# Regrouping VectorE's attention steps, output projections in rounds, and paired norms of 256 columns, in a three-layer block on one core

## The reference

```python
# layers 0 and 1
u = rms_norm(x) @ w_in                     # 256 x 2560
# layer 0: retention, 6 heads;  layer 1: differential attention, 6 heads of 2 maps
p = softmax(q k^T * scale + bias);  a = p[0] - lam * p[1];  o = a @ v
o_mem = memory_attention(...)              # 4 heads of 64, keys from mem
x = x + concat([o_main, o_mem]) @ w_out    # 1024 x 1024
x = x + (silu(gate) * up) @ w_down         # 2816 wide
# layer 2 (the second block): an SSD mixer and a "fox" attention side by side
y_ssd = ssd_mixer(...)   # 16 heads of 64: scores = (C B^T) * decay, times x * dt
y_fox = fox_mixer(...)   # 16 heads of 64: q and k normed per head, causal softmax, @ v
x = x + concat([y_ssd, y_fox]) @ w_out     # 2048 x 1024, then a convolved gated MLP
```

## Time and profile before

| | before |
|---|---|
| median of 3 runs | 1086.97 us (1084.75 to 1086.97) |
| profiled execution, its own time | 1086.96 us |
| its span, first to last instruction | 1085.1 us |
| PE busy | 1049.3 us, 97% |
| DVE / ACT / POOL busy | 761.3 / 587.0 / 176.6 us |
| mean granted TensorE clock | 0.995 |
| chain that ended last | PE 81%, DVE 12%, ACT 3% |

### The profile page before, as it was taken

One profiled execution on the slowest core, in us unless ns is written; L12 is line 12 of the kernel. 1 busy time (PEld: TensorE's weight loads), 2 busy tenths in 40 slices (PEclk: granted clock), 3 DMA queues, 4 the chain that ended last, 5 costly groups with the idle time before them and its releaser, 6 DMA issues.

```text
span 1085.1 us, 23877 instructions
## 1 busy us (share of the span) xinstructions
PE 1049.3 (97%) x8638; PEld 1011.4 (93%) x8638; DVE 761.3 (70%) x1324; ACT 587.0 (54%) x1047; POOL 176.6 (16%) x184
## 2 busy tenths in 40 slices
PE   6999999999999997999999999999899999999998
PEld 6989899999999886899999998999788999999998
DVE  6876685666555887876666548868877679988843
ACT  7654564444545654654445446665555466666532
POOL 3100121111010000411111110000211033444300
PEclk9999999999999999999999999999999999999999
DMA  8533455555665421555555664544233355555563
GB/s 291 176 131 108 142 176 179 184 183 173 191 179 175 135 85 54 180 189 176 188 177 170 193 198 140 175 136 137 83 113 91 124 194 177 191 175 187 165 204 104
DMA packets 51479, 174.43 MB, mean 161 GB/s; under 512 B 5840, under 2 KB 7120, under 8 KB 51280
## 3 DMA queue, kind: packets, MB, share of 16 engines
q1 hardware_dynamic: 51408, 173.46, 49.4%
HBM read 172.39 MB, written 1.05 MB: 160 GB/s over the span
## 4 chain that ended last, share of the span: by engine, by line
PE 81%; DVE 12%; ACT 3%; issue 2%; POOL 1%; DMA 1%; SPq 0%; DVEq 0%; ACTq 0%; POOLq 0%
PE bank L685 24%; PE bank L686 23%; PE bank L687 23%; DVE ring_lo L1482 4%; DVE xw_lo L1488 1%; PE bank L668 1%; PE bank L670 1%; PE bank L669 1%; ACT tmp L1239 1%; ACT tmp L1298 1%; PE bank L802 1%; DMA ring_raw<-w_kv 1%; DVE x L1580 1%; PE bank L793 0%; DVE tmp L1855 0%
## 5 line engine op out<-in xcount | busy, mean ns | idle before, releaser
L685 PE MATMUL bank<-xw_hi,ring_hi 128*128 128x256 f32 x1576 | 453.3, 288 | 2.7 <-DVE ring_lo L1482 1.5
L686 PE MATMUL bank<-xw_lo,ring_hi 128*128 128x256 f32 x1576 | 446.4, 283 | 0.0
L687 PE MATMUL bank<-xw_hi,ring_lo 128*128 128x256 f32 x1576 | 446.3, 283 | 0.0
L1482 DVE TENSOR_TENSOR ring_lo<-ring_raw,ring_hi 128x1024 fp32r<-128x1024 f32 (+2 forms) x338 | 402.4, 1194 | 56.5 <-ACT ring_hi L1057 50.8
L1057 ACT ACTIVATE ring_hi<-ring_raw 128x1024 fp32r<-128x1024 f32 (+2 forms) x338 | 341.1, 1012 | 88.8 <-PE bank L687 84.7
L685 PEld LDWEIGHTS bank<-xw_hi,ring_hi 128*128 128x128 f32 x1576 | 302.6, 192 | 9.8 <-issue 5.1
L686 PEld LDWEIGHTS bank<-xw_lo,ring_hi 128*128 128x128 f32 x1576 | 302.7, 192 | 0.2
L687 PEld LDWEIGHTS bank<-xw_hi,ring_lo 128*128 128x128 f32 x1576 | 302.7, 192 | 0.0
L685 PE MATMUL bank<-act_hi,ring_hi 128*128 128x256 f32 x736 | 212.1, 288 | 12.2 <-DVE ring_lo L1898 7.8
L686 PE MATMUL bank<-act_lo,ring_hi 128*128 128x256 f32 x736 | 210.1, 285 | 0.0
L687 PE MATMUL bank<-act_hi,ring_lo 128*128 128x256 f32 x736 | 210.0, 285 | 0.0
(11 more groups left out here) (199 smaller groups left out, 1168.8 us busy)
## 6 DMA issues: line engine op xcount, KB each, us to landing
ring_raw<-w_up SPq DMA_DIRECT2D x132, 512.0 KB, 3.2
ring_raw<-w_in SPq DMA_DIRECT2D x85, 512.0 KB, 3.3
ring_raw<-w_down SPq DMA_DIRECT2D x48, 512.0 KB, 3.7
ring_raw<-w_down SPq DMA_DIRECT2D x24, 384.0 KB, 3.8
ring_raw<-w_ob SPq DMA_DIRECT2D x10, 512.0 KB, 3.5
ring_raw<-w_oa SPq DMA_DIRECT2D x16, 256.0 KB, 2.7
ring_raw<-w_oa SPq DMA_DIRECT2D x8, 512.0 KB, 3.6
ring_raw<-w_kv SPq DMA_DIRECT2D x7, 512.0 KB, 6.3
```

The lines of the kernel that those rows point to most:

```text
L685: mm(bank[b][:, 0:T], w_hi, tile(hi, t), start=kk == 0, stop=False)
L686: mm(bank[b][:, 0:T], w_hi, tile(lo, t), start=False, stop=False)
L687: last = mm(bank[b][:, 0:T], w_lo, tile(hi, t), start=False, stop=end)
L1482: V.tensor_tensor(ring_lo[:, a:b], ring_raw[:, a:b], ring_hi[:, a:b].bitcast(f32), SUB).then_inc(lo_done, 1)
```

## The change

- **Output projection in rounds (layers 0 and 1).** `oa` and `ob` become one stage `oc` of eight full slots. A slot is a pair of inputs and a half (four) of the output tiles, in the order of `ROUNDS`. All eight outputs accumulate in banks 0 to 3 (two to a bank) until the fourth pair; then `x` is added once, 512 columns at a time (`rounds_into_stream`). Half 1 uses banks 2 and 3, and waits for the last scores.
- **Differential softmax (layer 1).** VectorE no longer scales the second map: it folds the factors into one small operation and makes the difference in one pass; ScalarE applies the common factor.
- **Memory and fox outputs.** ScalarE copies them from PSUM straight to `act_hi` and VectorE writes `act_lo` from PSUM, in place of a VectorE copy, a ScalarE copy and a GpSimd subtraction. Their `mix` steps go.
- **Fox softmax (layer 2).** Two reductions over both heads in place of four (banks 2 and 3 become one tensor `scores2`); ScalarE normalises in place of VectorE.
- **SSD weights.** The time step is multiplied into `x_tok` in two operations (`ssd_steps`); then one product for a pair of heads replaces four smaller ones.
- **Query and key norms of layer 2.** A query pair and a key pair share one chain of 256 columns (`pair_squares`, `pair_norm`, `pair_spread`, `pair_out`); fox scores start one slot later.

The diff, cut to its core:

```diff
 PHASES = [("kv", 8, [8], 4),
-          ("in0", 20, [8], 20), ("oa0", 8, [6], 8), ("ob0", 2, [8], 2), ("up0", 44, [8], 4), ("down0", 24, [8, 8, 6], 12),
-          ("in1", 20, [8], 20), ("oa1", 8, [4], 8), ("ob1", 4, [8], 4), ("up1", 44, [8], 4), ("down1", 24, [8, 8, 6], 12),
+          ("in0", 20, [8], 20), ("oc0", 8, [8], 8), ("up0", 44, [8], 4), ("down0", 24, [8, 8, 6], 12),
+          ("in1", 20, [8], 20), ("oc1", 8, [8], 8), ("up1", 44, [8], 4), ("down1", 24, [8, 8, 6], 12),
           ("in2", 45, [8], 45), ("oa2", 16, [8, 4], 16), ("ob2", 4, [8], 4), ("up2", 44, [8], 4), ("down2", 24, [8, 8, 6], 12)]
...
+ROUNDS = {"oc0": [(0, 0), (1, 0), (0, 1), (1, 1), (2, 0), (3, 0), (2, 1), (3, 1)],
+          "oc1": [(0, 0), (1, 0), (0, 1), (1, 1), (2, 0), (2, 1), (3, 0), (3, 1)]}
...
-    norm(1, 23, 10 + 64, True)
+    norm(1, 22, 10 + 64, True)
...
-    for k, slot in ((6, 11), (7, 11), (0, 19), (1, 19), (2, 23), (3, 23), (4, 26), (5, 26)):
+    for k, slot in ((0, 19), (1, 19), (2, 23), (3, 23), (4, 25), (5, 25)):
...
+        at(2, a + 2, "ssd_weights", p)
         for n in range(2):
-            at(2, a + n + 1, "ssd_weights", 2 * p + n)
             at(2, a + n, "ssd_decay", 2 * p + n)
+    at(2, 16, "ssd_steps", 0)
+    at(2, 18, "ssd_steps", 1)
     for j in range(4):
         a = 21 + 6 * j
-        norm(2, a + 2, 20 + 2 * j)
-        norm(2, a + 4, 28 + 2 * j)
+        at(2, a + 2, "pair_squares", j, 0)
+        at(2, a + 4, "pair_squares", j, 1)
+        at(2, a + 5, "pair_norm", j)
+        for which in range(2):
+            plan[2][a + 6 + which].insert(0, ("pair_spread", j, which))
+            plan[2][a + 7 + which].insert(0, ("pair_out", j, which))
         for n in range(2):
-            p, slot = 2 * j + n, a + 7 + 3 * n
+            p, slot = 2 * j + n, a + 8 + 3 * n
             at(2, slot, "fox_scores", p)
             plan[2][slot + 1].insert(0, ("fox_probs", p))
             at(2, slot + 2, "fox_weights", p)
             at(2, slot + 3, "fox_values", p)
-            at(2, slot + 4, "mix", 8 + p)
...
+        def mixed(layer, k):
+            if layer < 2 and k >= 6:
+                return sm_out, number["fill", (layer, 12 + k)] + 1
+            if layer == 2 and k >= 8:
+                return fx_out, k - 7
+            return mix_lo, number["mix", (layer, k)] + 1
...
+            def project_rounds(layer, then, halfway):
+                ph = PH[f"oc{layer}"]
+                for c, (pair, half) in enumerate(ROUNDS[ph.name]):
+                    slot, g = ph.tile(0, c)
+                    pe.wait_ge(lo_done, g + 1)
+                    if pair == 0 and half == 1:
+                        if layer == 0:
+                            pe.wait_ge(sm_e, 4)
+                            pe.wait_ge(r_pt, RET_HEADS)
+                        else:
+                            pe.wait_ge(sm_m, so_far["scores"])
...
+                        if pair == 3 and j == 1:
+                            last.then_inc(ob_done, 1)
+                    last.then_inc(tile_done, 1)
+                    then(c)
...
+            def rounds_into_stream(layer, q, after):
+                ph = PH[f"oc{layer}"]
+                for c, (pair, half) in enumerate(ROUNDS[ph.name]):
+                    split_hi(ph, 0, c)
+                    after(ph, 0, c)
+                    if pair == 3:
+                        for p in (2 * half, 2 * half + 1):
+                            act.wait_ge(out_ready, ph.out0 + p + 1)
+                            stream_hi(q, 2 * p, x)
+                            stream_hi(q, 2 * p + 1, x)
+                            stream_square(q, 2 * p, x)
+                            stream_square(q, 2 * p + 1, x)
...
+            def softmax(layer, kind, h, m):
+                if kind != "diff" or m == 0:
+                    return
+                n = number["scores", (layer, kind, h, m)]
+                act.wait_ge(diffed, h + 1)
+                p, c0 = probs(n), 2 * ((n - 1) % 2)
+                for it, (a, width) in enumerate([(0, P), (P, T)]):
+                    last = A(p[:, a:a + width], p[:, a:a + width], ACT.Copy, scale=rrow[:, c0 + it:c0 + it + 1])
+                last.then_inc(sm_d, 1)
+            def values(layer, kind, h):
+                t, full = filled(layer, kind, h)
+                if kind != "mem" or not full:
+                    return
+                act.wait_ge(sm_o, number["weights", (layer, kind, h)] + 1)
+                A(tile(act_hi, t - 12), bank[6][:, 0:T], ACT.Copy).then_inc(vals_hi, 1)
...
+            def fox_probs(layer, p):
+                act.wait_ge(fx_r, p + 1)
+                for n in range(2):
+                    for it, (a, width) in enumerate([(0, P), (P, T)]):
+                        w_ = fox_p(n)[:, a:a + width]
+                        last = A(w_, w_, ACT.Copy, scale=rrow[:, 2 * n + it:2 * n + it + 1])
+                last.then_inc(fx_n, 1)
+            def fox_values(layer, p):
+                act.wait_ge(fx_o, p + 1)
+                A(tile(act_hi, 8 + p), bank[6][:, 0:T], ACT.Copy).then_inc(fx_hi, 1)
...
+            def rounds_into_stream(layer, q, early, middle, late):
+                ph = PH[f"oc{layer}"]
+                late_split = []
+                for c, (pair, half) in enumerate(ROUNDS[ph.name]):
+                    early(ph, 0, c)
+                    if pair == 3:
+                        for p in (2 * half, 2 * half + 1):
...
+                            two_out = x[:, 2 * p * T:(2 * p + 2) * T]
+                            V.tensor_tensor(two_out, two_out, bank[p][:, :], ADD).then_inc(out_ready, 1)
+                            stream_lo(q, 2 * p, x)
+                            stream_lo(q, 2 * p + 1, x)
+                    middle(ph, 0, c)
+                    late_split.append(c)
+                    if not (c == 6 and pair == 3):
+                        for d in late_split:
+                            split_lo(ph, 0, d)
+                        late_split = []
+                    late(ph, 0, c)
...
+            def pair_norm(layer, j):
+                n, y = pair_no(j), normed(0)[:, 0:T]
+                v = newton_step(n, y)
+                V.scalar_tensor_tensor(y, v, -3.0, y, ADD, MUL).then_inc(np_nt, 1)
+                dve.wait_ge(np_nt, 5 * n + 3)
+                dve.wait_ge(np_bc, PAIRS_FROM + 2 * j)
+                root_split(n, y, T)
+            def pair_out(layer, j, which):
+                dve.wait_ge(np_bc, PAIRS_FROM + 2 * j + which + 1)
+                t = 20 + 8 * which + 2 * j
+                V.scalar_tensor_tensor(u[:, t * T:(t + 2) * T], u[:, t * T:(t + 2) * T], pcol(("foxq", "foxk")[which]),
+                                       bank[4][:, :], MUL, MUL).then_inc(np_out, 1)
...
-                    small_op(V.tensor_scalar(rrow[:, c:c + 2], rrow[:, c:c + 2], lam[:, 4:5], None, MUL))
-                    small_op(*[V.tensor_scalar(p[:, a:a + width], p[:, a:a + width], rrow[:, c + it:c + it + 1], None, MUL)
-                               for it, (a, width) in enumerate([(0, P), (P, T)])])
                     first, c0 = probs(n - 1), 2 * ((n - 1) % 2)
+                    small_op(V.scalar_tensor_tensor(rrow[:, c:c + 2], rowsum[:, c0:c0 + 2], lam[:, 4:5], rrow[:, c:c + 2],
+                                                    MUL, MUL))
                     for it, (a, width) in enumerate([(0, P), (P, T)]):
-                        last = V.scalar_tensor_tensor(p[:, a:a + width], first[:, a:a + width],
-                                                      rrow[:, c0 + it:c0 + it + 1], p[:, a:a + width], MUL, ADD)
-                    last.then_inc(sm_n, 1)
+                        last = V.scalar_tensor_tensor(p[:, a:a + width], p[:, a:a + width],
+                                                      rrow[:, c + it:c + it + 1], first[:, a:a + width], MUL, ADD)
+                    last.then_inc(diffed, 1)
...
+            def ssd_weights(layer, p):
+                if p == 0:
                     dve.wait_ge(cb_done, 2)
-                dve.wait_ge(ss_e, h + 1)
-                g = h // 8
-                for tt, (a, width) in enumerate([(0, T), (T, P)]):
-                    k = 16 * tt + h
-                    last = V.scalar_tensor_tensor(s[:, a:a + width], s[:, a:a + width], tok_dt[:, k:k + 1],
-                                                  cb[:, g * 384 + a:g * 384 + a + width], MUL, MUL)
-                last.then_inc(ss_p, 1)
+                dve.wait_ge(ss_e, 2 * p + 2)
+                s = ssd_pair(p).rearrange("p (n c) -> p n c", n=2)
+                g = p // 4
+                V.tensor_tensor(s, s, cb[:, g * 384:(g + 1) * 384].unsqueeze(1).to_broadcast([P, 2, 384]), MUL).then_inc(ss_p, 1)
+            def ssd_steps(layer, g):
+                if g == 0:
+                    dve.wait_ge(act_small, 7)
+                    dve.wait_ge(tr_out, so_far["turn"])
+                xg = x_tok[:, :].rearrange("p (t h d) -> p t h d", t=2, h=16)[:, :, 8 * g:8 * g + 8, :]
```

(18 more changed lines are left out.)

210 lines of the change are left out of this document (148 added, 62 removed).

## The result

The changed kernel takes 1089.76 us (median of 7 runs, 1088.53 to 1090.69); the kernel before takes 1086.97 (median of 7, 1084.07 to 1087.40). The ratio over all these executions is 1.0034, with a 95% interval of 1.0022 to 1.0046 (the medians alone give 1.0026): 0.34% slower, where 1.0% faster was forecast. The profiled execution took 1090.28 us.

A forecast was written before the change was run, and what follows sets the result against it. TensorE's steady matmul stream was taken as the bound, leaving about 18 us of PE waits and 5 us of clock falls; gains less tail and other costs sum to -10.7 us from 1086.96, giving 1076.3 us, range 1072 to 1081.

The forecast's parts named there:

- Heads of the rounds (-1.1, -1.7): Layer 0's first round needs only inputs 6 and 7: `act_lo` wait gone, -1.1 us, and the clock's fall behind it, -1.7.
- Layer 1 up to the rounds (-1.7, -0.9): Scalings off VectorE remove PE's 1.71 us wait, -1.7 us; the bank 0 wait at 424 us falls from 2.3 to 1.4, -0.9.
- Rounds of layer 1 (-3.4): Slots of 2.9 us for 1.44 cover attention steps: softmax -1.5, both `root_parts` -1.4, `act_lo` -0.5, in all -3.4 us.
- half of the last `act_lo`: Layer 1's rounds: of the 1.0 us wait for the last `act_lo`, half goes, -0.5 us.
- The tails (+3.9, +0.7): A half's outputs all finish in the last pair, so PE waits for chains and mean square: layer 1 +3.9 us, layer 0 +0.7.
- one fall in layer 1, called moved: Layer 1's clock fall was taken as moved from 424 us to the tail, not gone, so not counted in the sum.
- Layer 2 (-5.0, -1.7, +1.0, -1.3, +0.3, +0.2): Multiply waits -5.0 us, clock fall at 778 us -1.7, slot 29 +1.0, spreading -1.3, longer fox chain +0.3, pair product +0.2.
- a sign of being wrong: Prediction called itself wrong if tails cost nothing or much more, ScalarE's copies showed as PE's releaser, or `ssd_steps` appeared in PE's waits.
- the 1.0 us that it put at slot 29: Layer 2: first fox scores read the second `pair_out` at once, behind an SSD product, +1.0 us.
- The spreading: Layer 2: a pair has four 256-column matmuls (0.48 us) for two chains' eight of 128 (0.80): -1.3 us over 4 pairs.
- The slower rival: ScalarE becomes the late engine in layer 2, a copy holding the next decay; 1092 us at 2 us per head pair; chance 0.09.
- The clock as a whole: Of three clock falls, those in layers 0 and 2 go, -1.7 us each; layer 1's moves to its tail.

The follow-up runs named there:

- run 9: Changed kernel with layers 0 and 1's out projections again in two stages, without rounds, as in the kernel before: 1084.34 us, ratio 0.9997 to the kernel before.
- run 4: Changed kernel with layer 1's split of inputs 2 and 3 one slot earlier (22 for 23): 1086.48 us, ratio 0.9991 to the kernel before.
- Runs 3: Changed kernel with 45 unread matmuls added in PE's pauses in the first up tiles of layers 0 and 1: 1085.49 us, ratio 1.0008 to the kernel before.
- 11: Changed kernel with norm step first, earlier split of inputs 2 and 3, scaling and maxima as before, no unread matmuls: 1077.22 us, ratio 0.9924 to the kernel before.
- run 1: Changed kernel with layer 2's pair norm step put ahead of the fox scores in its slots: 1084.40 us, ratio 0.9989 to the kernel before.
- run 6: Changed kernel with layer 2's row maxima again taken head by head, in four reductions: 1085.19 us, ratio 0.9992 to the kernel before.
- run 8: Changed kernel with norm step first, earlier split of inputs 2 and 3, unread tail matmuls, fox scaling on VectorE, maxima head by head: 1073.66 us, ratio 0.9897 to the kernel before.

## Why the prediction was wrong

- **Heads of the rounds (-1.1, -1.7): the wait right, the fall credited too surely.** No wait for `act_lo` and full clock at 120 us. But a longer fall came in the tail, and run 9, which has the wait back, had no fall behind it in its profile.
- **Layer 1 up to the rounds (-1.7, -0.9): right.** Measured -3.2 for -2.6; the wait at the first round is 1.24 us for 1.4 forecast.
- **Rounds of layer 1 (-3.4): the mechanism right, one term missed.** The wait for the softmax fell to 0.5 us and those for the parts went; the 1.44 us slots were the cause (run 9 has them back). The split of inputs 2 and 3 was costed at "half of the last `act_lo`"; it was 2.0 us and a fall of the clock. I looked at when the inputs are computed, not at where ScalarE's copy stands (run 4).
- **The tails (+3.9, +0.7): waits nearly right, the clock in layer 0 left out.** 2.9 and 2.8 us of waits in place of 3.9 and 2.1, but the stretches grew by 5.6 and 4.5. I had one fall in layer 1, called moved, which makes the forecast 5.6 there: the same number, from a longer wait and a shorter fall. In layer 0 I had none. Runs 3 and 11 show that the falls come of the tails' pauses and price the two together at 2.8 and 2.9 us.
- **Layer 2 (-5.0, -1.7, +1.0, -1.3, +0.3, +0.2): this is the step that failed.** "With half as many chains, each wait has a slot or more to spare" was said of the number of chains and not of the queue that a chain's seed stands in. The seed stood behind a softmax in its own slot, and that softmax had been lengthened at the front by wide maxima. The waits from 720 us on rose by 2.3 us (9.2 for 6.9), and there were two falls for one. ScalarE's copies did appear as PE's releaser (1.7 us in three waits), which the prediction had named as a sign of being wrong; the 1.0 us that it put at slot 29 did not come. The spreading did save about what it should: by the distances of their starts its matmuls take 2.5 us for 3.5, the averages 2.3 for 2.9. Mending the order in the slot (run 1) or the wide maxima (run 6) is enough alone to bring layer 2 under the kernel before (by 2.6 and 1.9 us). With both, and the scaling back on VectorE, it is 6.4 us shorter, close to the forecast's 6.5. That is luck in part: the forecast rested on the scaling being gone from VectorE, and in run 8 it is there.
- **The slower rival** named ScalarE as the late engine in layer 2. The place is right and the engine's order too; what it held up was the seed, three times, and not a decay or a copy at each of eight heads. The copies were sized nearly right (1.49 us for four at 840.25 and 852.07, 1.3 taken). The row of 1.32 us that the prediction set beside its estimate of 1.39 is of wider copies, though, and was no close check.
- **The clock as a whole.** The forecast took two of three falls as removed (-3.4 us); the profile has five, two of them twice as long. It also priced a fall too high: at 1.2 GHz matmuls start every 0.21 us and not every 0.12 (from 424.41 to 426.54 us the kernel before has ten such steps), and the 15 or so of one short fall cost 1.4 us, not 1.7.
- **Where the 14.0 us went** that lie between forecast and profiled execution (1090.28 - 1076.3). By the table, layer 2 has 9.3 of them, the two tails 5.5 and the rounds of layer 1 1.1; the heads gave 2.5 back, and the rest lies at the two ends. Of layer 2's 9.3, about 6 are waits (+2.3 where the terms for waits make -3.5) and 3 the two falls where none was forecast.

What stays open: whether run 6 was spared the fall at 812 us by its shorter waits or by chance, since falls differ between executions (below).
